# Chunked delta rule: decays by one exp, keys turned ahead, a factor moved to step 1, activation tables kept between the halves

## The reference, cut to what matters

```
qkv = silu(causal_depthwise_conv(qkv, conv_b_w)); q, k = l2_normalize(q), l2_normalize(k)
beta = sigmoid(beta_raw); g = -exp(a_log) * softplus(a_raw + dt_bias)
gc = cumsum(g)                                      # within a chunk
decay = exp(where(incl, gc[i] - gc[j], -inf))
low = where(strict, (k * beta) @ k.T * decay, 0)
sol = solve(low + I, [v * beta, k * beta * exp(gc)])
attn = q @ k.T * decay
per chunk: v_new = u - w @ S; o = (q * exp(gc)) @ S + attn @ v_new
           S = S * exp(gc_last) + (k * exp(gc_last - gc)).T @ v_new
```

## Time and profile before

| | |
|---|---|
| median of 3 runs | 905.26 us (905.05 to 905.57) |
| profiled execution | 906.0 us |
| its span | 904.2 us |
| PE busy | 883.5 us (98% of the span) |
| DVE, ACT, POOL busy | 459.9, 504.7, 668.4 us |
| clock granted to PE | 1.0 of full speed |

### The profile page before, as it was taken

One profiled execution on the slowest core, in us unless ns is written; L12 is line 12 of the kernel. 1 busy time (PEld: TensorE's weight loads), 2 busy tenths in 40 slices (PEclk: granted clock), 3 DMA queues, 4 the chain that ended last, 5 costly groups with the idle time before them and its releaser, 6 DMA issues.

```text
span 904.2 us, 18970 instructions
## 1 busy us (share of the span) xinstructions
PE 883.5 (98%) x7503; PEld 816.2 (90%) x7503; DVE 459.9 (51%) x979; ACT 504.7 (56%) x712; POOL 668.4 (74%) x480
## 2 busy tenths in 40 slices
PE   6999999999999999999999999999899999999997
PEld 6999999999997889999999999888897899998886
DVE  4368863485531633777768776635556442220004
ACT  5775543763336456565667656566556355664331
POOL 5986766457656888857776776769786579989882
PEclk9999999999999999999999999999999999999999
DMA  8663543435444556545444454456552356656531
GB/s 316 207 219 130 162 130 132 126 108 166 141 131 167 179 186 183 192 137 166 142 139 134 150 164 159 146 174 207 168 162 94 94 160 221 205 198 207 198 118 46
DMA packets 40824, 146.08 MB, mean 162 GB/s; under 512 B 4512, under 2 KB 4640, under 8 KB 40736
## 3 DMA queue, kind: packets, MB, share of 16 engines
q1 hardware_dynamic: 39296, 140.71, 47.5%
q10 hardware_dynamic: 1440, 4.16, 1.4%
HBM read 143.81 MB, written 1.05 MB: 160 GB/s over the span
## 4 chain that ended last, share of the span: by engine, by line
PE 90%; DVE 3%; ACT 2%; issue 2%; POOL 2%; DMA 1%; DVEq 0%; SPq 0%; ACTq 0%; POOLq 0%
PE dense L510 25%; PE dense L511 24%; PE dense L512 24%; PE bank L871 2%; POOL wlo L485 1%; PE dense L566 1%; PE bank L708 1%; POOL wlo L484 1%; PE bank L709 1%; DVE cv L1717 1%; DMA raw<-weight_units_dram 1%; PE bank L903 1%; PE bank L857 1%; PE bank L1014 1%; PE bank L512 1%
## 5 line engine op out<-in xcount | busy, mean ns | idle before, releaser
L485 POOL TENSOR_TENSOR wlo<-raw,whi 128x512 fp32r<-128x512 f32 (+1 forms) x259 | 408.9, 1585 | 22.8 <-ACT whi L1131 22.7
L1131 ACT ACTIVATE whi<-raw 128x1024 fp32r<-128x1024 f32 (+1 forms) x262 | 273.4, 1057 | 232.8 <-PE dense L512 199.3
L484 POOL TENSOR_TENSOR wlo<-raw,whi 128x512 fp32r<-128x512 f32 x195 | 253.5, 1300 | 182.8 <-ACT whi L1131 180.8
L510 PE MATMUL dense<-x_hi,whi 128*128 128x256 f32 x1232 | 349.9, 284 | 10.6 <-DVE wlo L1648 8.2
L511 PE MATMUL dense<-x_lo,whi 128*128 128x256 f32 x1232 | 342.8, 278 | 0.0
L512 PE MATMUL dense<-x_hi,wlo 128*128 128x256 f32 x1232 | 342.6, 278 | 0.0
L510 PEld LDWEIGHTS dense<-x_hi,whi 128*128 128x128 f32 x1232 | 232.5, 189 | 14.7 <-issue 8.1
L511 PEld LDWEIGHTS dense<-x_lo,whi 128*128 128x128 f32 x1232 | 232.8, 189 | 0.7 <-issue 0.2
L512 PEld LDWEIGHTS dense<-x_hi,wlo 128*128 128x128 f32 x1232 | 232.9, 189 | 0.0
L510 PE MATMUL dense<-whi,ya_hi 128*128 128x512 f32 x192 | 77.4, 403 | 1.0 <-issue 0.8
L512 PE MATMUL dense<-whi,ya_lo 128*128 128x512 f32 x192 | 75.0, 391 | 0.0
(11 more groups left out here) (336 smaller groups left out, 1374.6 us busy)
## 6 DMA issues: line engine op xcount, KB each, us to landing
raw<-weight_units_dram SPq DMA_DIRECT2D x261, 512.0 KB, 3.8
xtok<-in_x_dram SPq DMA_DIRECT2D x1, 1024.0 KB, 7.3
gb<-in_ln_g_dram ACTq DMA_DIRECT2D x2, 512.0 KB, 5.1
gb<-in_ln_b_dram ACTq DMA_DIRECT2D x2, 512.0 KB, 7.3
out_dram<-zt SPq DMA_DIRECT2D x3, 256.0 KB, 2.0
qT<-x_turned_dram SPq DMA_DIRECT2D x2, 256.0 KB, 4.6
raw<-weight_units_dram SPq DMA_DIRECT2D x2, 256.0 KB, 5.5
qT<-x_turned_dram SPq DMA_DIRECT2D x1, 512.0 KB, 7.3
```

The costliest lines, as they stand in the source:

```text
L484: pool.tensor_tensor(wlo[:, slot, 0:half], unit_slot(u)[:, 0:half], whi[:, slot, 0:half].bitcast(F32), ALU.subtract)
L485: pool.tensor_tensor(wlo[:, slot, first:2 * half], unit_slot(u)[:, first:2 * half], whi[:, slot, first:2 * half].bitcast(F32), ALU.subtrac ...
L510: pe.matmul(out_, lh, rh, start=start, stop=False, skip_group_check=True)
L1131: act.activation(whi[:, u % NSPL, first:], unit_slot(u)[:, first:], ACT.Copy).then_inc(hi_done, 1)
```

## The change

- Step 0 makes the differences in one orientation only, into bank B; ACT's exp goes from B into `AT`, and serves both products.
- Keys are turned ahead of a half (`key_transposes`, at n = 14 and n = 41). ACT squares the turned keys into `LT`, DVE adds each row of them (`tensor_reduce`), and the multiplications by ones, their copies and the Square of each pair are gone. The bank pair of k and q is freed after the convolution of q. In step 0, DVE scales the turned keys into `KX`, which it did in step 3.
- The row factor enters in step 1, in four `scalar_tensor_tensor` of 128x128 with a negated factor as the per-partition scalar. Step 1 makes query by key products in the other orientation, and step 3 turns `AT` back in place of the keys.
- `gate_products` makes `GAF` with eight `tensor_scalar` of 128x128 in place of two `tensor_tensor` of 128x512.
- `gates` adds to the numbers in the bank itself. DVE copies the gate sums at n = 15, and ACT takes exp of the copy at n = 16.
- The blank unit blocks are written one unit after a half has started. After step 20 of half 0 the tables stay as they are.

```diff
+KEYS_BEHIND = (14, 41)
...
+            def key_transposes(half):
+
+                if half == 0:
+                    pe.wait_ge(rest_loaded, 16)
+                else:
+                    pe.wait_ge(gdn_vector, dve_step(0, 19, 1))
+                    pe.wait_ge(gdn_squares, 2)
+                pe.wait_ge(conv_silu, 3 * (2 * half + 1) + 1)
+                for g in range(2):
+                    for u in range(4):
+                        last = pe.transpose(SB[2 * g][:, u * P:(u + 1) * P], kT[:, 4 * half + u, g * P:(g + 1) * P], ident)
+                    last.then_inc(k_turned, 1)
...
                         if half == 0:
-                            pe.wait_ge(gate_exp, 1)
+                            pe.wait_ge(gate_taken, 1)
...
+                        pe.wait_ge(gdn_exp, 3 * half + g + 1)
...
                         if s == 0:
-                            pe.matmul(A[:, o], upto, unit(GAF[:, g, :], u), start=True, stop=True)
-                            last = pe.matmul(B[:, o], unit(GAF[:, g, :], u), upto, start=True, stop=True)
+                            last = pe.matmul(B[:, o], upto, unit(GAF[:, g, :], u), start=True, stop=True)
                         elif s == 1:
                             pe.matmul(A[:, o], kT[:, h, tok], kT[:, h, tok], start=True, stop=True)
-                            last = pe.matmul(B[:, o], kT[:, h, tok], qT[:, h, tok], start=True, stop=True)
+                            last = pe.matmul(B[:, o], qT[:, h, tok], kT[:, h, tok], start=True, stop=True)
...
-                            pe.transpose(A[:, o], kT[:, h, tok], ident)
+                            pe.transpose(A[:, o], unit(AT[:, g, :], u), ident)
...
-                if n < FIRST_YA and n % 8 == 5:
-                    k_sums_of(n // 8)
+                if n in KEYS_BEHIND:
+                    key_transposes(KEYS_BEHIND.index(n))
...
-                if part == "k":
-                    act.activation(cv[:, 0, :].rearrange("p (h t) -> p h t", h=2), dst, ACT.Square).then_inc(k_squares, 1)
-                    settle(k_squares)
...
+            def key_squares(half):
+
+                for g in range(2):
+                    act.wait_ge(k_turned, 2 * half + g + 1)
+                    act.activation(LT[:, g, :], SB[2 * g][:, :], ACT.Square).then_inc(k_squares, 1)
+                    settle(k_squares)
...
-                        link(act.activation(A[:, :], A[:, :], ACT.Exp))
-                        act.activation(B[:, :], B[:, :], ACT.Exp).then_inc(gdn_exp, 1)
+                        act.activation(AT[:, g, :], B[:, :], ACT.Exp).then_inc(gdn_exp, 1)
...
-                    if s in (2, 20):
+                    if s == 2 or (half, s) == (1, 20):
                         tables(SILU_TABLES)
...
             def gate_products(half):
                 for g in range(2):
-                    link(vec.tensor_tensor(four(GAF[:, g, :]), all4(after), heads(g, 5, half), ALU.mult), gdn_gates if g else vec_chain)
+                    for u in range(4):
+                        link(vec.tensor_scalar(GAF[:, g, u * P:(u + 1) * P], after, gt[:, 5, g, 4 * half + u:4 * half + u + 1], None, ALU.mult),
+                             gdn_gates if g and u == 3 else vec_chain)
...
+            def key_sums(half):
+
+                for g in range(2):
+                    vec.wait_ge(k_squares, 2 * half + g + 1)
+                    link(vec.tensor_reduce(kn[:, 0, g, 4 * half:4 * half + 4], four(LT[:, g, :]), AX_X, ALU.add), k_taken)
...
                     if s == 0:
-                        vec.wait_ge(gdn_exp, 3 * half + g + 1)
-                        link(vec.tensor_tensor(four(EL[:, g, :]), four(A[:, :]), heads(g, 8, half), ALU.mult))
-                        vec.tensor_tensor(four(AT[:, g, :]), four(B[:, :]), all4(upto), ALU.mult).then_inc(gdn_vector, 1)
+                        vec.tensor_tensor(four(KX[:, g, :]), four(A[:, :]), heads(g, 6 + g, half), ALU.mult).then_inc(gdn_vector, 1)
...
-                        link(vec.scalar_tensor_tensor(EL[:, g, :], A[:, :], -1.0, EL[:, g, :], ALU.mult, ALU.mult))
+                        vec.wait_ge(gdn_exp, 3 * half + g + 1)
+                        for u in range(4):
+                            cols, h = slice(u * P, (u + 1) * P), 4 * half + u
+                            link(vec.scalar_tensor_tensor(EL[:, g, cols], A[:, cols], gt[:, 0, g, h:h + 1], AT[:, g, cols], ALU.mult, ALU.mult))
...
+                if n == KEYS_BEHIND[0] + 1:
+                    vec.wait_ge(gate_sums, 1)
+                    link(vec.tensor_copy(gt[:, 6, :, :], SB[3][:, 0:2 * GH].rearrange("p (t h) -> p t h", t=2)), gate_taken)
+                if n - 1 in KEYS_BEHIND:
+                    key_sums(KEYS_BEHIND.index(n - 1))
```

More of the change, by code:

```diff
@@ L305, in build @@
         gate_sums = sem("gate_sums")
-        gate_exp = sem("gate_exp")
+        gate_taken = sem("gate_taken")
         xhi_done = sem("xhi_done")
@@ L314, in build @@
         k_squares = sem("k_squares")
-        k_sums = sem("k_sums")
+        k_turned = sem("k_turned")
         k_taken = sem("k_taken")
@@ L674, in gd_dense @@
                 wide_unit(half, pair_of(group, p)[1 if part in ("gd_q", "gd_z") else 0], x_hi, x_lo).then_inc(split_used, 1)
-            def k_sums_of(p):
-                if p == 0:
+            def key_transposes(half):
+                if half == 0:
                     pe.wait_ge(rest_loaded, 16)
[L680 to L686, removed]
+                else:
[6 more added lines that the diff above has]
+                    last.then_inc(k_turned, 1)
             def gate_sums_of():
@@ L1203, in conv_taps @@
                     act.wait_ge(columns_loaded, 16)
-                if p > 0 and part == "k":
-                    act.wait_ge(k_sums, p)
                 for i in range(2):
@@ L1332, in _ @@
                     gdn(1, 0)
+                if n in KEYS_BEHIND:
+                    key_squares(KEYS_BEHIND.index(n))
+                if n - 1 in GDN_FIRST:
+                    blank(GDN_FIRST.index(n - 1))
                 for j in range(KT):
@@ L1346, in _ @@
                     if n + 1 == GDN_FIRST[0]:
-                        act.wait_ge(gate_sums, 1)
-                        act.activation(gt[:, 6, :, :], SB[3][:, 0:2 * GH].rearrange("p (t h) -> p t h", t=2), ACT.Exp).then_inc(gate_exp, 1)
-                        settle(gate_exp)
+                        act.wait_ge(gate_taken, 1)
+                        link(act.activation(gt[:, 6, :, :], gt[:, 6, :, :], ACT.Exp))
                     key_norms(GDN_FIRST.index(n + 1))
-                    blank(GDN_FIRST.index(n + 1))
                     if n + 1 == GDN_FIRST[1]:
@@ L1718, in conv @@
                          conv_done if back == 3 else vec_chain)
-            def take_k_sums(p):
-                vec.wait_ge(k_sums, p + 1)
-                link(vec.tensor_copy(kn[:, 0, :, 2 * p:2 * p + 2].rearrange("p t h -> p h t"),
-                    pair_of("gd_kq", p)[0][:, 0:4].rearrange("p (h t) -> p h t", h=2)), k_taken)
-                free("gd_kq", p)
+            def key_sums(half):
+                for g in range(2):
+                    vec.wait_ge(k_squares, 2 * half + g + 1)
+                    link(vec.tensor_reduce(kn[:, 0, g, 4 * half:4 * half + 4], four(LT[:, g, :]), AX_X, ALU.add), k_taken)
             def gate_factors(half):
@@ L1732, in gate_factors @@
                 link(vec.tensor_tensor(gt[:, 8, :, hh], gt[:, 2, :, hh], kn[:, 3, :, hh], ALU.mult))
+                link(vec.tensor_scalar(gt[:, 0, :, hh], gt[:, 8, :, hh], -1.0, None, ALU.mult))
                 link(vec.tensor_tensor(gt[:, 7, 1, hh], gt[:, 6, 1, hh], gt[:, 8, 1, hh], ALU.mult))
@@ L1752, in gdn @@
                         vec.wait_ge(gdn_level, 2 * half + g + 1)
+                    elif s == 0:
+                        vec.wait_ge(k_turned, 2 * half + g + 1)
                     else:
@@ L1778, in gdn @@
                     elif s == 3:
-                        link(vec.tensor_tensor(four(KX[:, g, :]), four(A[:, :]), heads(g, 6 + g, half), ALU.mult))
+                        link(vec.tensor_tensor(four(AT[:, g, :]), four(A[:, :]), all4(upto), ALU.mult))
                         vec.tensor_tensor(four(VB[:, g, :]), four(B[:, :]), heads(g, 3, half), ALU.mult).then_inc(gdn_vector, 1)
@@ L1884, in _ @@
                     r = n - 8 * p
-                    if r == 6:
-                        take_k_sums(p)
                     if 2 <= r < 8:
                         conv(p, "kqv"[(r - 2) // 2], r % 2)
+                    if r == 5:
+                        free("gd_kq", p)
                 if n == 12:
                     gates()
+                if n == KEYS_BEHIND[0] + 1:
[3 more added lines that the diff above has]
+                    key_sums(KEYS_BEHIND.index(n - 1))
                 if n == GDN_FIRST[1]:
```

2 lines of the change are left out of this document (1 added, 1 removed).

## The result

The changed kernel took 920.88 us (median of 4 runs: 920.88, 910.85, 921.12, 920.88); the kernel before, beside it, 905.15 us (4 runs, 904.55 to 905.57). The ratio is 1.0143, with a 95% interval of 1.0112 to 1.0174. That is 1.4% slower, and beyond the range of the forecast (909.6, 899.5 to 912.5). The profiled execution is one of the 920.88.

What follows compares the result with a forecast made beforehand. PE, busy 98% of the span, was taken as the bound. PE work -5.0, stalls -1.3, step 1 +1.7, the eight's waits +7.3 and +1.6 gave +4.3 us on 905.3: 909.6, range 899.5 to 912.5.

Steps and rivals of the forecast that it cites:

- the sum itself: Whole kernel: -4.6 us without hold-ups, +7.3 in half 0 and +1.6 in half 1 give +4.3 us.
- ACT misses the Square: Half 0: ACT no longer does a Square of 0.63 us, part of why DVE reaches `GAF` about 1.1 us earlier.
- The eight `tensor_scalar`: `GAF` at n = 14 and n = 25: each takes a turn with POOL, about 1.35 us; three run in a gap at n = 25.
- The stalls behind the eight: PE waits 5.3 us at step 0 of half 0, 2 more in steps 1 and 2, 1.6 at half 1's step 6.
- What goes from PE: First layer: fewer step 0 products (-3.6) and sums of squared keys (-3.2), sixteen more transposes (+1.75): -5.0 us.
- Stalls that go: PE's waits for the bank pair (-0.26), step 0 of half 0 (-0.56) and step 1 of half 1 (-0.49): -1.3 us.
- no wait ends there: Half 1's step 0: DVE's scaling of keys, two instructions of 0.7 in place of four, ends no wait.
- Step 1 on DVE: Four 128x128 instructions per g, 1.5 us against 0.7; covered in half 0, +1.7 us in half 1 (bounds 0 and 1.8).
- Other edits at nothing: Key squares and reductions at n = 14 and the new order at n = 41 have about 2 us of cover: no cost.
- the order at n = 41: Step 20's tables come some 2 us later, covered; as a rival it delays half 1's step 0 2 to 3 us, 0.04.
- they run free: Rival: the eight need no turn with POOL, 0.3 us each, so the sum stays -4.6: 900.7 us; chance 0.37.

Runs made afterwards that it cites:

- e12: The changed kernel with the Square of the first pair's keys put back on ACT, its result read by nothing: 911.38 us, ratio 1.0062.
- e7b: The changed kernel with `tail_lo` and half 1's `GAF` on POOL, half 0's eight written to a PSUM bank and copied to SBUF: 905.34 us, ratio 0.9998.
- e4: The changed kernel with both `tail_lo` and `GAF` made by POOL: 904.97 us, ratio 0.9984.
- e10: The changed kernel with `GAF` on POOL, `tail_lo` still on DVE, and the first keys' Square put back on ACT, unread: 903.3 us, ratio 0.998.

## Why the prediction missed

- **The step that failed** is the sum itself, which lacks a term: the Squares of the keys are counted only as time that ACT wins ("ACT misses the Square"). It didn't ask what an earlier ACT does to the instruction of two SBUF operands at n = 7, and its sum gives every such instruction one turn of POOL, although had one of 16 numbers held up for 1.95 us, from 52.05 to 54.00. That is through the POOL instruction of that moment and the whole of the next, the last of POOL's row (kernel before):

```profile
52.69 1.28 POOL L485 TENSOR_TENSOR wlo<-raw,whi 128x512 fp32r<-128x512 f32 x1
```

  What the runs showed in its place is a `tail_lo` that stands for 11.10 us and a PE that waits 7.9 us for it at n = 8 and then has half its clock; the price is 9.8 us.
- **The eight `tensor_scalar`**: right in kind, and nearly in size. Forecast 1.35 us each, measured 1.26 (changed) and 1.18 (e12). The free price shows as well: at n = 25 four of the eight fell into a gap of POOL, in 1.25 us together, 0.3 each, where the forecast had three.

```profile
115.07 1.25 DVE L1693 TENSOR_SCALAR GAF<-con,gt 128x128 f32<-128x128 f32 x4
```

  In the Trainium skill, "SBUF — State Buffer", "Who interferes with whom", the lock lasts one instruction and goes to whoever issues first. The eight, and e7b with its output in a bank, agree; a `tail_lo` that stands through eight to ten whole instructions of POOL does not follow from it.
- **The stalls behind the eight.** In e12, which is the change without the loss at n = 7, PE waits 5.3 us at step 0, as forecast. In the three places behind it and at n = 25 it waits another 0.73 + 0.97 + 0.47 + 0.82 + 0.34 = 3.3 us against 3.6, but that agreement is in part luck: the 0.97 and the 0.47 stand in e4 too, which has no eight, and e10, which has none either, waits 0.41 us at the second of them.
- **A second term that the sum lacks** is the clock. Behind the wait at step 0 of e12 PE's granted clock was 0.50 until 71.1 us; the row of e12 above has the 16 starts of step 0 in 3.49 us, and e10, which doesn't wait there, has them in 1.95:

```profile
63.69 1.95 PE L768 MATMUL bank<-GAF,con 128*128 128x128 f32 x16
```

  That is 1.5 us for a wait that the sum priced at its own length.
- **The forecast as a whole**: 909.6 for a kernel without the loss at n = 7; e12 took 911.38, and 5.9 us more than before, where +4.3 was worked out. The 1.6 us between them are about what the clock took. That the changed kernel is slower came out as forecast, but of its 15.7 us the forecast's own reason makes up only these 5.9. e12 less e10 is 8.1 us, against the 8.9 forecast for the eight.
- **What goes from PE**: -5.0 forecast; PE's busy time is 883.5 before and 878.9 in e10, -4.6.
- **Stalls that go**: two of three. The bank pair (0.26) and step 0 (0.56) don't wait in e10. Step 1 of half 1, which was to lose its 0.49, waits 1.27 us: the row of `gate_factors` now stands between ACT's norms and the scaled keys, and each of its instructions waits for POOL, 4.4 us for four in the changed kernel (191.03 to 195.45). The prediction says of the scaling behind them that "no wait ends there".
- **Step 1 on DVE**: the four take 1.51 us, as forecast, and are not held up: one input is in a bank. The added stall was to be 1.7; step 2 of half 1 waits 1.28 us in e10 against 0.80, as PE had already been stopped at step 1. The two steps of half 1 together came out as forecast (+1.2: -0.49 and +1.7; measured 1.6 us of waiting before and 2.9 in e10, by PE's starts), but for another reason, which is luck. Both rows are of e10:

```profile
178.32 0.46 PE L770 MATMUL bank<-kT 128*128 128x128 f32 x2 [1.27 <-issue]
...
186.60 0.33 PE L773 MATMUL bank<-con,EL 128*128 128x128 f32 x1 [1.28 <-DVE AT L1788]
```

- **Other edits at nothing**: wrong for the factors (above, and 0.38 us at step 1 of half 0 in e10); right for the order at n = 41, where no wait shows.
- **The rival "they run free"** forecast 900.7. With both hold-ups taken away the change gave 903.3 (e10) and 904.97 (e4); only with the factors and step 1 moved as well did it come to 900.89.

## What to carry to other kernels

Where VectorE and GpSimd share a stretch, list every VectorE instruction with two SBUF inputs, and every `tensor_scalar` or copy from SBUF to SBUF, however small, and price each at one GpSimd instruction at least, and at the rest of GpSimd's row at worst; splitting one into eight multiplies the waits. Where TensorE then waits for several microseconds, add the half clock behind the wait (1.5 us behind 5.3 us here, 2.6 behind 7.9). Give such work to GpSimd itself (0.2 to 0.4 us for the small ones here) or put one end in PSUM. And when an edit takes work off an engine that feeds GpSimd, look at whether GpSimd loses its gaps: here a kernel with an idle 0.1 to 0.5 us ahead of the row was never shut out, and one without it was in many of its runs.

## What the runs showed of the hardware

- Beside a row of GpSimd instructions without a gap, one 128x128 subtraction on VectorE waited 11.0 to 12.8 us, until the row ended, in some runs of the same kernel and not in others; with an earlier gap in the row it took 1.06 to 1.10 us in every profile.
- A `tensor_scalar` of 128x128 took 1.26 us from SBUF to SBUF beside a busy GpSimd and 0.3 us in a gap of GpSimd; from SBUF to PSUM it took 0.37 us beside a busy one. GpSimd's instructions beside the eight took 1.29 us, as without them.
- TensorE stood still for 7.9 us and then had half its clock (0.50, 1.2 GHz) for the next 5.7 us (changed); it stood still for 5.3 us and then had it for the next 3 us (e12).
